# Samples' stage and merge of a hybrid decoder step: when ring units and merge weights are requested, when o is split, where the gate rows and the SiLU stand

## The reference, cut to what matters

```
u = rms_norm(x) @ w_in                                    # 544 x 2048 @ 2048 x ~11.9k
o_a = rwkv7(u_a) * silu(g)                                # 544 x 1024
o_b = nsa(q, compressed, selected, window) * silu(g_b)    # 544 x 1024
merged = sigmoid(m_a) * (o_a @ w_pa) + sigmoid(m_b) * (o_b @ w_pb)
y = rms_norm(x + merged @ w_o)
```

## Time and profile before

| | |
|---|---|
| median of three runs | 2326.49 us |
| the profiled execution's own time | 2317.33 us |
| its span | 2315.7 us |
| PE busy | 2212.3 us (96%) |
| DVE, ACT, POOL busy | 1258.6, 815.9, 280.2 us |
| mean granted TensorE clock | 0.978 of full speed |

### The profile page before, as it was taken

One profiled execution on the slowest core, in us unless ns is written; L12 is line 12 of the kernel. 1 busy time (PEld: TensorE's weight loads), 2 busy tenths in 40 slices (PEclk: granted clock), 3 DMA queues, 4 the chain that ended last, 5 costly groups with the idle time before them and its releaser, 6 DMA issues. The chain is left out here.

```text
span 2315.7 us, 53115 instructions
## 1 busy us (share of the span) xinstructions
PE 2212.3 (96%) x22026; PEld 2027.1 (88%) x22026; DVE 1258.6 (54%) x2503; ACT 815.9 (35%) x1512; POOL 280.2 (12%) x430
## 2 busy tenths in 40 slices
PE   7999999999999999999999899999899898999997
PEld 6998888888888888999999887878888787999997
DVE  6344555555555554377888367765134453554454
ACT  5334333342433332222222345544223332433342
POOL 0000000000000000011100525211304331000000
PEclk8999999999999999999999999999999999999999
DMA  4321221212222121387775623311839974445564
GB/s 149 101 85 53 63 79 55 67 54 67 68 63 77 58 81 53 120 297 256 247 240 181 194 64 102 103 58 56 274 113 308 308 263 159 149 152 166 185 204 137
DMA packets 139396, 318.92 MB, mean 138 GB/s; under 512 B 28074, under 2 KB 56852, under 8 KB 138132
## 3 DMA queue, kind: packets, MB, share of 16 engines
q1 hardware_dynamic: 99556, 219.25, 29.7%
q0 software_dynamic: 17040, 55.63, 7.2%
q10 hardware_dynamic: 22560, 40.64, 5.2%
HBM read 277.70 MB, written 46.06 MB: 140 GB/s over the span
## 5 line engine op out<-in xcount | busy, mean ns | idle before, releaser
L209 PE MATMUL acc<-xh,w_hi 128*128 128x272 f32 x2944 | 654.8, 304 | 12.6 <-DVE w_lo L175 11.6
L209 PE MATMUL acc<-xh,w_lo 128*128 128x272 f32 x2944 | 613.6, 290 | 0.0
L209 PE MATMUL acc<-xl,w_hi 128*128 128x272 f32 x2944 | 613.3, 290 | 0.0
L209 PEld LDWEIGHTS acc<-xh,w_hi 128*128 128x128 f32 x2944 | 462.6, 190 | 66.6 <-issue 43.2
L209 PEld LDWEIGHTS acc<-xl,w_hi 128*128 128x128 f32 x2944 | 467.9, 191 | 0.0
L209 PEld LDWEIGHTS acc<-xh,w_lo 128*128 128x128 f32 x2944 | 466.0, 191 | 0.0
L175 DVE TENSOR_TENSOR w_lo<-w_raw,w_hi 128x1024 fp32r<-128x1024 f32 x174 | 212.4, 1223 | 249.0 <-ACT w_hi L168 242.6
L168 ACT ACTIVATE w_hi<-w_raw 128x1024 fp32r<-128x1024 f32 x198 | 208.9, 1056 | 314.3 <-PE acc L209 205.9
L1335 DVE SCALAR_TENSOR_TENSOR b_C<-b_rows,b_pos_s,b_C 128x512 f32<-128x512 f32 x240 | 162.4, 744 | 0.0
L1040 PEld LDWEIGHTS rbank<-m 64*64 64x64 f32 x3840 | 120.2, 135 | 22.0 <-issue 14.2
L1040 PE MATMUL rbank<-m 64*64 64x64 f32 x3840 | 132.3, 220 | 0.0
(11 more groups left out here) (474 smaller groups left out, 3435.9 us busy)
## 6 DMA issues: line engine op xcount, KB each, us to landing
w_raw<-in_w_all SPq DMA_DIRECT2D x168, 512.0 KB, 3.6
b_rows<-in_cmp_rows SPq DMA_DIRECT2D x128, 256.0 KB, 3.7
m_w<-in_w_mo SPq DMA_DIRECT2D x44, 512.0 KB, 4.0
w_raw<-in_w_mo SPq DMA_DIRECT2D x42, 512.0 KB, 3.9
w_raw<-in_w_all ACTq DMA_DIRECT2D x20, 512.0 KB, 5.4
tmp_uT<-ub ACTq DMA_DIRECT2D x35, 272.0 KB, 3.2
d_ring<-in_sel_k SPq DMA_DIRECT2D x64, 128.0 KB, 4.1
d_ring<-in_sel_k POOLq DMA_DIRECT2D x64, 128.0 KB, 4.4
```

The source lines that it names most:

```text
L209: ins = self.nc.tensor.matmul(acc[:, c, 0:HALF], w[:, k % KH, :], x[:, k, c * HALF:(c + 1) * HALF], start=(k == 0 and m == 0), stop=(k == ...
```

## The change

Six edits. (1) The load of `bias` moves behind the third ring unit, and ring unit t (0 to 5) waits on SP and on POOL until half h0+1+t has been multiplied. (2) The gate rows' product and reduction move from place 40 to place 32 (`GATES_AT`). (3) The split of o is due from place 94 in steps of 0.25 (DVE 0.125 later), before from 91 in steps of 0.5 (DVE 0.25 later). (4) ACT loads the weights of merge halves 10 and 11 in the tail of the samples' stage, into the two `w_raw` buffers; the merge's ring of raw buffers is renumbered (`raw_of`), SP starts with gate rows 8 and 9, and ACT waits at the stage's end for the two loads. (5) SiLU stands in units 10 and 11, the turning of o in units 12 to 15 (before 11 to 14). (6) `finish(n-1)` goes ahead of `silu_half` and the turned tiles.

```diff
-O_HIGH_AT = X_LOWER_FREE + 3
+O_HIGH_AT = LAST_PROJECTED - 2
+GATES_AT = SAMPLE_START - 8
@@ attend_samples
-    W.h_ahead = W.h_load = PROJECTED + N_EARLY + 2
+    W.h_ahead, W.h_load = PROJECTED + N_EARLY + 2, PROJECTED + N_EARLY + 2 + N_RAW
@@ SP
-            sp.dma_start(bias[:, :], A["bias_s"]).then_inc(bias_in, 16)
             sp.wait_ge(table_in, 16)
             for t in range(N_RING):
+                sp.wait_ge(W.half_done, W.h0 + 2 + t)
                 load_unit(sp, t, 0)
+                if t == 2:
+                    sp.dma_start(bias[:, :], A["bias_s"]).then_inc(bias_in, 16)
@@ POOL
             for t in range(N_RING):
+                pool.wait_ge(W.half_done, W.h0 + 2 + t)
                 load_unit(pool, t, 1)
@@ ACT
-                    at_o = O_HIGH_AT + 0.5 * o_highs[0] if o_highs[0] < KW + 1 else LATER
+                    at_o = O_HIGH_AT + 0.25 * o_highs[0] if o_highs[0] < KW + 1 else LATER
+            for h in range(W.h_ahead, W.h_load):
+                act.wait_ge(W.w_in[h % N_RAW], 16 * (h // N_RAW + 1))
@@ DVE
-                    at_o = O_HIGH_AT + 0.5 * o_lows[0] + 0.25 if o_lows[0] < KW + 1 else LATER
+                    at_o = O_HIGH_AT + 0.25 * o_lows[0] + 0.125 if o_lows[0] < KW + 1 else LATER
-            background(SAMPLE_START)
+            background(GATES_AT)
             dve.wait_ge(gates_spread, 1)
...
             dve.sem_inc(gates_set, 1)
+            background(SAMPLE_START)
@@ merge_and_out
+        raw_of = lambda x: (x - N_EARLY - N_RAW) % N_RING_M
-        TURN_AT = N_EARLY + 3
+        TURN_AT = N_EARLY + 4
+        SILU_AT = N_EARLY + 2
-            weights(X0)
-            merge_gates(N_EARLY)
-            weights(X0 + 1)
-            merge_gates(N_EARLY + 1)
-            for x in range(X0 + 2, X0 + N_RING_M):
+            for n in range(N_EARLY, N_EARLY + 2):
+                merge_gates(n)
+            for x in range(X0 + N_RAW, X0 + N_RING_M):
                 weights(x)
@@ ACT
-                if 1 <= n - N_EARLY < 3:
-                    q = n - N_EARLY - 1
+                if 0 <= n - SILU_AT < 2:
+                    q = n - SILU_AT
@@ DVE
-                if 1 <= n - N_EARLY < 3:
-                    silu_half(n - N_EARLY - 1)
+                if n > N_EARLY:
+                    finish(n - 1)
+                if 0 <= n - SILU_AT < 2:
+                    silu_half(n - SILU_AT)
...
-                if n > N_EARLY:
-                    finish(n - 1)
```

More of the change, by code:

```diff
@@ L2822, in weights @@
                     src = A["w_mo"][N_OUT + u % N_OUT][:, k * KW:(k + 1) * KW, :]
-                sp.dma_start(w[x % N_RING_M][:, :, :], src).then_inc(w_in[x % N_RING_M], 16)
+                sp.dma_start(w[raw_of(x)][:, :, :], src).then_inc(w_in[raw_of(x)], 16)
             def merge_gates(n):
@@ L2886, in high_part @@
             def high_part(x):
-                act.wait_ge(w_in[x % N_RING_M], 16 * ((x - X0) // N_RING_M + 1))
+                if x >= X0 + N_RAW:
+                    act.wait_ge(w_in[raw_of(x)], 16 * ((x - X0) // N_RING_M + (raw_of(x) >= N_RAW)))
                 if x >= N_EARLY + N_RING_M:
                     act.wait_ge(half_done, x - N_RING_M - N_EARLY + 1)
-                f(w_hi[x % N_RING_M][:, :, :], w[x % N_RING_M][:, :, :], ACT.Copy).then_inc(w_hi_done, 1)
+                f(w_hi[x % N_RING_M][:, :, :], w[raw_of(x)][:, :, :], ACT.Copy).then_inc(w_hi_done, 1)
             def sigmoid(n):
@@ L2945, in low_part @@
                 j = x % N_RING_M
-                v.tensor_tensor(w_lo[j][:, :, :], w[j][:, :, :], w_hi[j][:, :, :].bitcast(F32), ALU.subtract)\
+                v.tensor_tensor(w_lo[j][:, :, :], w[raw_of(x)][:, :, :], w_hi[j][:, :, :].bitcast(F32), ALU.subtract)\
                     .then_inc(w_lo_done, 1)
```

## The result

The changed kernel takes 2292.51 us (median of four runs, 2289.94 to 2300.47), the kernel before 2322.75 beside it; the ratio is 0.9873, with a 95% interval of 0.9836 to 0.991. The profiled execution has a span of 2288.3 us, before 2315.7: 27.4 us less, where the sum of the prediction was 27.0. I measured both traces from mark to mark, with marks that every one of the kernels here has: ACT's evacuations of chunks 81 and 86, DVE's first small job, PE's arrival at Tn of pairs 2 and 3 (start less idle time), the merge's first matmul, the first square sum.

The account below looks back on a forecast made before the run. PE, 96% busy, bounds the kernel, so time comes only from its waits and half clock. 12.2 + 7.2 + 1.5 + 6.1 = 27.0 us off the 2326.5 median gives 2299.5, shaded to 2298; range 2283 to 2309.

Parts of the forecast that it names:

- A: Stage's start, evacuations of chunks 81 to 86: spreading ring units and bias gains 12.2 us, between 6.8 and 13.9.
- The step of bounding the ten loads: ACT's q and kN loads at the stage's start: end after 8.3 us at q's rate, or at 1656.9 as before.
- The bound of 4.5 us: Stage's start: PE's wait for half 168 if ACT's ten loads keep the rate of before; about 4.5 us.
- B: Gate rows at place 40: moving their product to place 32 removes wait and half clock; gains 7.2 us, between 5.4 and 7.2.
- the lower bound: Gate rows: 5.4 us gained if oa's 16 matmuls of 32 columns don't depend on the clock.
- C: Tn(2) to Tn(3), o split later: saves 8.8 us, new wait for ninth low part costs 7.3; gains 1.5 us.
- D: Merge's start, first matmul to first square sum: finish earlier and gate row 10 earlier gain 6.1 us, between 2.4 and 8.8.
- The moved weight loads: Two loads moved into the samples' tail: cost nothing, 1.3 us if the second is as slow as beside ring units.
- the ninth low part: Rival at tile 7, pair 2: the ninth low part is no wait; o split gains 8.8 us, time 2291; chance 0.14.
- ACT's ten loads: Rival at the stage's start: the ten loads stay slow; gain there 6.8 us, time 2304; chance 0.13.
- The gate row: Rival at the merge's start: gate row 10 comes no earlier; gain there 2.4 us, time 2303; chance 0.09.
- Slower weight loads over more halves: Rival, halves 165 to 170 and on: ring units delay weight loads, landings from 19 us decide; time 2345; chance 0.02.

Follow-up runs that it names:

- r1: Kernel before with only the ring units each waiting for a half and bias behind the third unit: 2305.54 us against 2323.04, ratio 0.9931.
- r6: Changed kernel with the split of o due from 91 in steps of 0.5 again: C 51.5 us; executed once.
- r10: Changed kernel with ninth low part before select(3), gate rows 10 and 11 before ob_t, K3's background call at 107: 2273.43 us against 2321.29, ratio 0.9797.
- r2: Kernel before with only the bias load moved behind the third ring unit, all six units still asked for at once: A 73.85 us; executed once.
- r11: Kernel before with ACT issuing half 169's weight load ahead of its ten small loads: A 73.0 us; executed once.
- r3: Kernel before with only the gate rows moved to place 32: 2312.43 us, ratio 0.9959; B 4.85 us.
- r4: Kernel before with only the split of o due from 94 in steps of 0.25: C 50.7 us; executed once.
- r8: Changed kernel with DVE's o split steps 0.23 for 0.25, putting the ninth low part ahead of select(3): 2280.71 us against 2324.16, ratio 0.9819.
- r7: Changed kernel with weights of merge halves 10 and 11 loaded by SP at the merge's start again: D 166.1 us; executed once.
- r9: Changed kernel with gate rows 10 and 11 asked for ahead of ob_t at the merge's start: D 159.4 us; executed once.
- r5: Kernel before with only finish(n-1) moved ahead of silu_half and the turned tiles: D 163.7 us; executed once.

## Why the prediction was right

It was right in its time's range, its sign and all four places. The sum of 27.0 against 27.4 us of span is closer than its terms: the medians differ by 30.2 us (2298 was forecast, 2292.51 came), and A read from other executions is 2 to 3 us larger. Point by point:

- *A, 12.2 predicted, 12.5 measured.* That agreement is luck in part. The kernel before was read in its quickest execution of this stretch (74.1 us, others 76.0 to 76.8), the changed one in its slowest (61.6 without the product, others 60.2 to 60.9): the means are 75.7 and 60.7, a gain of 15.0, above the bound of 13.9. The step of bounding the ten loads gave 8 to 11 us, the trace 8.2. The wait left was put at 1.7 us; it is 1.1 here and 0 to 0.4 in r1 and r6 to r10. The bound of 4.5 us at the rate of before was too low, since it left out the 2.46 us in which ACT issues the load of half 169 ahead of the evacuation; that bound never came into play. The account of the loss was half right. I said that ACT is held up by its ten loads; r2 shortened these to 9.1 us and gained nothing. What r1 shows is that asking for one unit per half is enough. The DMA engines' busy share is not the cause by itself: it was 1.00 before and 0.99 in the changed kernel beside the same loads of kN. What edit 1 changed is how much had been asked for at once. r11 doesn't tell slow issuing from order on ACT's queue. How that makes an issue slow was not measured.
- *B, 7.2 predicted, 7.1 measured.* r3 shows it alone. The 16 small matmuls of `oa` took 1.97 us at the full clock for 3.59 before, so the lower bound, by which they don't depend on the clock, is out.
- *C, 1.5 predicted, 2.0 measured.* The new wait was reckoned at 5.2 us and is 5.10; r4 shows that edit 3 alone makes it, r6 that the edit is a trade, r8 that the order before `select(3)` is its only cause, worth 6.9 us. Without either wait C is 42.3, so the old split cost 8.9 us (reckoned 8.8) and the new one 6.9 (reckoned 7.3): 5.1 of wait and 1.8 that is mostly the half clock behind it, put at 2.1. In r4 and r7, with waits of 5.9, the gain is 0.5 and 1.2.
- *D, 6.1 predicted, 7.95 measured.* `finish(10)` was reckoned 27.7 us after the first matmul and is there, to the tenth, but by two errors that cancel: the gate row came 0.8 us later than reckoned, and ACT and DVE took 0.8 less from it to `finish(10)`. The term that was mis-sized is PE's arrival: the turn of o, 16 small matmuls of 1.97 us, moves into unit 12 and stands ahead of the wait, so that 0.76 us are left of 1.9, and the half clock's share with it. r9 takes even this away. The runs r6 and r8, with the same merge, show 163.8 and 162.1 us for waits of 1.7 and 1.2. By the means of all kernels with the old merge (169.2) and with the changed one (162.0) the gain is 7.2.
- *The moved weight loads* were costed at nothing, and the barrier's wait is 2.7 us as before. The ring's last unit is asked for at piece 28 and not at 32, as the prediction has it; nothing hangs on that.
- *The size beside the median.* Between the executions the stretch before the samples' stage is between 1627.6 and 1635.8 us long, in code that none of the kernels here changes. That is the spread of the runs; the 9.2 us between profile and median before were no property of the profile, and both medians have since come closer to it.

The rivals: the ninth low part does wait (r4), and ACT's ten loads did not stay slow. The Trainium skill has a smallest size for line rate, 512 B ("DMA: Bandwidth & Descriptors", Specifications). It speaks of the transfer; the time of issuing doesn't follow from the size of the pieces in this case's traces, since the same kN loads took 4.62 us, 5.71 in r11 and 1.34 in the changed kernel. The gate row came 2.0 us earlier, of 2.8 reckoned. Slower weight loads over more halves did not happen: the two that ACT waited for in this stretch landed 8.2 and 8.6 us after they were issued, where the rival needed 19. With the engines still 1.05 busy from 1656 to 1676, PE ran at the full clock:

```profile
1656.00:1676.00 20.00, 18.90 (x151) 18.68 (x150) 4.90 (x4) 8.14 (x12) 6.99 (x13) 1.00 1.05 372
```

## What to carry to other kernels

When work is queued by due times, a due time means only its order against the calls that stand around it. Write down, for the last item of each moved series, which long job it falls behind, and price that job. Where one engine is bound, measure each loss from mark to mark and not by its wait, since the slow clock behind a wait can double it. Take a loss from more than one execution: A's was 2 to 3 us larger in three others than in the one the prediction was read from. And when many MB are asked for at once, try asking for less at a time first: here it gained 12.5 to 15 us, while moving one load of the many (r2) or one request on ACT's queue (r11) left A at 73.9 and 73.0 us.

## What the runs showed of the hardware

The clock after a wait is not decided by the length of the wait alone. Pair 3's Tn waits 2.18 us for ACT in most kernels here; behind it the granted clock was half in the changed kernel and full in r6, over three microseconds each:

```profile
1877.50:1880.50 3.00, 3.00 (x15) 3.00 (x14) 0.00 (x0) 2.78 (x9) 1.17 (x3) 0.50 0.94 292
```
```profile
1877.60:1880.60 3.00, 3.00 (x26) 3.00 (x25) 0.70 (x3) 2.82 (x9) 1.22 (x3) 1.00 0.85 252
```

That is the 1.5 us between 42.8 and 41.3 in the table. The barrier's 2.67 us did the same: clock 0.56 behind it in the changed kernel, 1.00 in r10:

```profile
1918.00:1921.00 3.00, 2.95 (x14) 2.98 (x15) 1.28 (x2) 2.76 (x3) 2.43 (x5) 0.56 0.63 199
```
```profile
1907.90:1910.90 3.00, 3.00 (x24) 3.00 (x25) 1.28 (x2) 2.57 (x3) 2.49 (x5) 1.00 0.64 200
```

And a shorter one, 1.16 us, was followed by matmul pairs of 0.82 us in r8, where 16 small matmuls of o's turn had gone just before it:

```profile
1932.68 1.97 PE L3050 MATMUL m_turn<-ident,m_sq 32*128 32x32 f32 x16
...
1935.80 0.82 PE L3062 MATMUL acc<-xh,w_hi 128*128 128x272 f32 x2 [1.16 <-DVE x_plain L2972]
```

The small matmuls don't decide it alone: in the changed kernel a wait of 0.76 us came behind the same 16, and pairs of 0.52 us followed. And the half clock can come late. In r5 PE waits 2.16 us at unit 12, until 1967.85; it then runs 1.6 us at nearly the full clock, and only then falls to half:

```profile
1967.80:1969.40 1.60, 1.55 (x12) 1.55 (x13) 1.53 (x3) 0.64 (x2) 0.00 (x0) 0.96 0.32 41
1969.40:1971.00 1.60, 1.60 (x9) 1.60 (x9) 1.36 (x2) 1.60 (x4) 0.00 (x0) 0.50 1.00 361
```

So the first matmuls behind a wait don't show whether it costs; the stretch from mark to mark does. In the merge D is 159.4 us without a wait for a gate product (r9). Beyond their own waits r7, r6 and r8 lost some 2.8, 2.7 and 1.5 us against that, the changed kernel 0.1.

So a term for the half clock belongs in a sum with both its ends, nothing and nearly 3 us for a wait of 1 to 4 us. What decides between them no run here shows.
